# An expert layer on one core: 64 of 256 tokens leave the dense sweep, their rows gathered by index

## The reference, cut to what matters

```python
def block(xb):                      # xb: 128 tokens x 1024
    q = (xb @ w_q).reshape(128, 8, 2, 128)
    s = jnp.einsum('thpd,hpkd->thpk', q, subkeys)            # 128 keys per half
    s1, i1 = lax.top_k(s[:, :, 0], 16)
    s2, i2 = lax.top_k(s[:, :, 1], 16)
    cand = (s1[..., :, None] + s2[..., None, :]).reshape(128, 8, 256)
    cidx = (i1[..., :, None] * 128 + i2[..., None, :]).reshape(128, 8, 256)
    top, pos = lax.top_k(cand, 16)
    idx = jnp.take_along_axis(cidx, pos, axis=-1)            # expert numbers
    g = jax.nn.softmax(top, axis=-1)
    ue, ve = u[idx], v[idx]                                  # rows of 1024
    act = gelu(jnp.einsum('td,thkd->thk', xb, ue))
    return jnp.einsum('thk,thkd->td', g * act, ve)
```

## Time and profile before

| | |
|---|---|
| median of 3 runs | 5376.34 us (5371.48 to 5377.14) |
| the profiled execution | 5365.48 us, span 5363.7 us |
| PE busy | 4796.7 us (89%) |
| DVE / ACT / POOL busy | 3541.7 (66%) / 2498.5 (47%) / 516.1 (10%) |
| moved | 862.62 MB, mean 161 GB/s |
| granted clock, mean | 0.936 |

### The profile page before, as it was taken

One profiled execution on the slowest core, in us unless ns is written; L12 is line 12 of the kernel. 1 busy time (PEld: TensorE's weight loads), 2 busy tenths in 40 slices (PEclk: granted clock), 3 DMA queues, 4 the chain that ended last, 5 costly groups with the idle time before them and its releaser, 6 DMA issues. The chain is left out here.

```text
span 5363.7 us, 94694 instructions
## 1 busy us (share of the span) xinstructions
PE 4796.7 (89%) x35838; PEld 4543.3 (85%) x35838; DVE 3541.7 (66%) x7839; ACT 2498.5 (47%) x4941; POOL 516.1 (10%) x789
## 2 busy tenths in 40 slices
PE   8868999999899999976799999969888988887896
PEld 6647999999899999964799999969778888886896
DVE  7554886588687668845587668846465555537564
ACT  6424554444455544432455444434454444446443
POOL 0000029000005700000005700000000000000000
PEclk9979999999999999988899999989878989978998
DMA  8402664766475467621375476635304444430453
GB/s 306 150 32 68 208 197 127 222 230 229 162 223 169 153 225 229 229 82 45 111 222 169 149 228 228 229 116 186 133 25 148 155 148 148 153 132 33 148 183 105
DMA packets 265098, 862.62 MB, mean 161 GB/s; under 512 B 29328, under 2 KB 32272, under 8 KB 264006
## 3 DMA queue, kind: packets, MB, share of 16 engines
q1 hardware_dynamic: 264070, 854.18, 48.8%
q10 hardware_dynamic: 576, 2.39, 0.1%
HBM read 805.03 MB, written 51.42 MB: 160 GB/s over the span
## 5 line engine op out<-in xcount | busy, mean ns | idle before, releaser
L148 DVE TENSOR_TENSOR weight_lo<-weight_ring,weight_hi 128x512 fp32r<-128x512 f32 x2840 | 1954.9, 692 | 1446.1 <-ACT weight_hi L141 1428.3
L141 ACT ACTIVATE weight_hi<-weight_ring 128x512 fp32r<-128x512 f32 x2840 | 1781.6, 631 | 2396.7 <-PE ffn_gu L173 269.9
L173 PE MATMUL ffn_gu<-second_x_hi,weight_hi 128*128 128x256 f32 x1408 | 399.0, 283 | 37.6 <-PEq L205 37.6
L173 PE MATMUL ffn_gu<-second_x_lo,weight_hi 128*128 128x256 f32 x1408 | 398.3, 283 | 0.0
L173 PE MATMUL ffn_gu<-second_x_hi,weight_lo 128*128 128x256 f32 x1408 | 398.0, 283 | 0.0
L173 PE MATMUL peer10e_dot<-peer_xh,weight_hi 128*128 128x256 f32 x1152 | 334.7, 291 | 13.6 <-PEq L205 9.9
L173 PE MATMUL peer00e_dot<-peer_xh,weight_hi 128*128 128x256 f32 x1152 | 334.6, 290 | 11.7 <-PEq L205 9.9
L173 PE MATMUL peer01e_dot<-peer_xh,weight_hi 128*128 128x256 f32 x1152 | 334.3, 290 | 11.9 <-PEq L205 9.9
L173 PE MATMUL peer00e_dot<-peer_xl,weight_hi 128*128 128x256 f32 x1152 | 326.7, 284 | 0.0
L173 PE MATMUL peer10e_dot<-peer_xl,weight_hi 128*128 128x256 f32 x1152 | 326.7, 284 | 0.0
L173 PE MATMUL peer00e_dot<-peer_xh,weight_lo 128*128 128x256 f32 x1152 | 326.6, 284 | 0.0
(11 more groups left out here) (612 smaller groups left out, 13529.4 us busy)
## 6 DMA issues: line engine op xcount, KB each, us to landing
weight_ring<-in_peer_tiles SPq DMA_DIRECT2D x768, 512.0 KB, 3.8
weight_ring<-in_w_tiles SPq DMA_DIRECT2D x652, 512.0 KB, 3.4
peer_acts<-peer00e_gelu SPq DMA_DIRECT2D x64, 256.0 KB, 4.2
peer00e_act_in<-peer_acts SPq DMA_DIRECT2D x64, 256.0 KB, 3.8
peer_acts<-peer01e_gelu SPq DMA_DIRECT2D x64, 256.0 KB, 4.1
peer01e_act_in<-peer_acts SPq DMA_DIRECT2D x64, 256.0 KB, 4.1
peer_acts<-peer10e_gelu SPq DMA_DIRECT2D x64, 256.0 KB, 4.1
peer10e_act_in<-peer_acts SPq DMA_DIRECT2D x64, 256.0 KB, 3.7
```

Of the source, the lines that this page charges most:

```text
L141: act.activation(self.hi[:, part % PARTS, :], self.ring[:, g % RING, (part % 2) * PART:(part % 2 + 1) * PART], ACT.Copy).then_inc(self.hi_ ...
L148: dve.tensor_tensor(self.lo[:, part % PARTS, :], self.ring[:, g % RING, (part % 2) * PART:(part % 2 + 1) * PART], self.hi[:, part % PARTS, ...
L173: last = pe.matmul(out, lhsT, rhs, start=start and i == 0, stop=stop and i == len(passes) - 1, **more)
```

## The change

- **64 tokens of each stream go another way.** The u and v sweeps take the other 192 (`DENSE`): matmuls of 192 moving columns, 48 groups. The 16 query tiles stay at 256.
- **Rows by index.** The 64 tokens lie twice over the 128 partitions, each copy with half of its 128 choices. After the routing of the first 128 tokens (which now comes first, 82 pieces from step 8) POOL fetches, by indirect DMA, one row of 1024 for each partition: 64 gathers from u, then 64 from v, into three buffers. DVE works on each in one pass of 1024 columns: a dot product with the token (`row`, i < 64), then, after a gelu on ACT, a multiply and add into `rows_sum`. Row i has its place at step `row_step(i)`, spread evenly to the end of the stage. PE adds up the two copies at the end (`fold`).
- **Coefficients on three engines.** POOL multiplies (`weigh`), ACT rounds, DVE takes the remainder. On POOL's queue the gathers, the one-hots and `weigh` are in one order; gather i waits until row i - 3 has been consumed.
- **One-hots**: the softmax weight moves to POOL's; DVE's is one operation of 512 columns a group instead of four of 128.
- **Splits per whole tile**, in all stages: one operation of 1024 columns each on ACT and DVE when PE is through with a tile's second part; three tiles (six parts) are kept.
- At the start of a stage the tokens' sum of hi and lo is written twice by DVE, turned by PE (8 transposes) and copied by ACT to `xt`.

```diff
-PARTS = 4
+PARTS = 6
...
+    def write_hi(self, act, g):
+        if g < len(self.tiles):
             act.wait_ge(self.arrived[g % RING], 16 * (g // RING + 1))
...
+            act.activation(self.tile_of(self.hi, g), self.ring[:, g % RING, :], ACT.Copy).then_inc(self.hi_done, 2)
+
+    def write_lo(self, dve, g):
+        if g < len(self.tiles):
+            dve.wait_ge(self.hi_done, 2 * g + 2)
+            dve.tensor_tensor(self.tile_of(self.lo, g), self.ring[:, g % RING, :],
+                              self.tile_of(self.hi, g).bitcast(F32), ALU.subtract).then_inc(self.lo_done, 2)
...
     def next_hi(self, act, part):
 
-        act.wait_ge(self.used, part + 1)
-        self.write_hi(act, part + PARTS)
+        if part % 2:
+            act.wait_ge(self.used, part + 1)
+            self.write_hi(act, part // 2 + PARTS // 2)
 
     def next_lo(self, dve, part):
 
-        self.write_lo(dve, part + PARTS)
+        if part % 2:
+            self.write_lo(dve, part // 2 + PARTS // 2)
...
+SPARSE = 64
+DENSE = T - SPARSE
+COPIES = P // SPARSE
+ROWS = 3
...
             def routing(step):
-                for c in range(QT):
-                    yield from choose(c)
                 for tt in range(2):
+                    for c in range(0, QT, 2):
+                        yield from choose(tt, c)
                     yield from top_k(tt, step)
-
-            def seconds(g):
+                    if tt == 0:
+                        yield from experts_of()
+                    routed_at.append(step())
...
+        def row_step(i):
+            lead = routed_at[0] + 14
+            return lead + i * (steps - 10 - lead) // (2 * NG) + (6 if i >= NG else 0)
+        def spread_step(g):
+            return routed_at[1] + 8 + g * (2 * front - 6 - routed_at[1] - 8) // groups
...
+                lo = SPARSE + g * GROUP
+                dve.tensor_tensor(second[:, g % 2, :, :], iota.unsqueeze(1).to_broadcast([P, GROUP, P]),
+                                  route[:, 1, lo:lo + GROUP].unsqueeze(2).to_broadcast([P, GROUP, P]),
+                                  ALU.is_equal).then_inc(second_done, 1)
+
+            def row(i):
+                dve.wait_ge(row_arrived[i % ROWS], 16 * (i // ROWS + 1))
+                here, j = rows[:, i % ROWS, :], i % NG
+                if i == 0:
+                    dve.wait_ge(xt_done, 1)
+                if i < NG:
+                    dve.tensor_tensor_reduce(here, here, xt[:, :], 1.0, 0.0, ALU.mult, ALU.add,
+                                             dots[:, j:j + 1]).then_inc(consumed, 1)
+                    return
+                dve.wait_ge(consumed, i)
+                if j == 0:
+                    dve.wait_ge(W.used, 2 * v0)
+                    dve.tensor_scalar(rows_sum, here, share[:, j:j + 1], None, ALU.mult).then_inc(consumed, 1)
+                else:
+                    dve.scalar_tensor_tensor(out=rows_sum, in0=here, scalar=share[:, j:j + 1], in1=rows_sum,
+                                             op0=ALU.mult, op1=ALU.add).then_inc(consumed, 1)
...
+            def rows_until(m):
+                while routed_at and done_rows[0] < 2 * NG and row_step(done_rows[0]) <= m:
+                    if done_rows[0] == NG:
+                        weigh_rows()
+                    row(done_rows[0])
+                    done_rows[0] += 1
+
             for m in range(2 * front):
                 now[0] = m
                 W.next_lo(dve, 2 * q0 + m)
-                if busy and m >= 4:
+                if busy and m >= 8:
                     busy = next(pieces, "done") != "done"
-                    if not busy:
-                        spread_from.append(m + 6)
-                if not busy and 0 <= m + 1 - spread_from[0] < groups:
-                    seconds(m + 1 - spread_from[0])
-            assert spread_from and spread_from[0] + groups + 4 <= 2 * front, spread_from
+                rows_until(m)
+                while not busy and done_groups[0] < groups and spread_step(done_groups[0]) <= m + 1:
+                    one_hots(done_groups[0])
+                    done_groups[0] += 1
+            assert not busy and done_groups[0] == groups
...
             def coef(j):
-                b, slot = j % 2, (j // 2) % ACTS_IN
-                if j == 0:
-                    dve.wait_ge(spread_out, groups)
-                if j % 2 == 0:
-                    dve.wait_ge(act_arrived[slot], 16 * (j // 2 // ACTS_IN + 1))
-                chain.mark(dve.tensor_tensor(weight[:, :], act_in[:, slot, j % 2, :], G[:, j, :], ALU.mult))
-                chain.wait()
-                if j >= 2:
-                    dve.wait_ge(W.used, 2 * (v0 + j - 2) + 2)
-                dve.tensor_copy(coef_hi[:, b, :], weight[:, :]).then_inc(weighed, 1)
-                dve.wait_ge(weighed, j + 1)
-                dve.tensor_tensor(coef_lo[:, b, :], weight[:, :], coef_hi[:, b, :].bitcast(F32),
+                dve.wait_ge(hi_done, j + 1)
+                dve.tensor_tensor(coef_lo[:, j % 2, :], weight[:, j % 2, :], coef_hi[:, j % 2, :].bitcast(F32),
                                   ALU.subtract).then_inc(weighted, 1)
-                dve.wait_ge(weighted, j + 1)
 
             coef(0)
             for m in range(2 * NKEYS):
                 if m % 2 == 0 and m // 2 + 1 < NKEYS:
                     coef(m // 2 + 1)
                 W.next_lo(dve, 2 * v0 + m)
+                rows_until(2 * front + m)
...
         @block.gpsimd
         def _(pool):
-            pool.wait_ge(routed, 2)
-            for g in range(groups):
+            def gather(i):
+                table, j = i // NG, i % NG
+                if i >= ROWS:
+                    pool.wait_ge(consumed, i - ROWS + 1)
+                pool.indirect_dma_start(rows[:, i % ROWS, :], None, (u_rows, v_rows)[table],
+                                        bass.IndirectOffsetOnAxis(ap=pick[:, table, j:j + 1].bitcast(U32), axis=0)
+                                        ).then_inc(row_arrived[i % ROWS], 16)
+
+            def one_hots(g):
+                if g == 0:
+                    pool.wait_ge(routed, 2)
                 if g >= 2:
                     pool.wait_ge(multiplied, g - 1)
                 for t in range(GROUP):
-                    at = g * GROUP + t
-                    last = pool.tensor_scalar(first[:, g % 2, t, :], iota, route[:, 0, at:at + 1], None, ALU.is_equal)
+                    lo = SPARSE + g * GROUP + t
+                    last = pool.tensor_scalar(first[:, g % 2, t, :], iota, route[:, 0, lo:lo + 1], route[:, 2, lo:lo + 1],
+                                              ALU.is_equal, ALU.mult)
                 last.then_inc(first_done, 1)
+
+            def weigh(j):
+                slot = (j // 2) % ACTS_IN
+                if j == 0:
+                    pool.wait_ge(spread_out, groups)
+                if j >= 2:
+                    pool.wait_ge(weighted, j - 1)
+                if j % 2 == 0:
+                    pool.wait_ge(act_arrived[slot], 16 * (j // 2 // ACTS_IN + 1))
+                pool.tensor_tensor(weight[:, j % 2, :], act_in[:, slot, j % 2, :], G[:, j, :], ALU.mult).then_inc(weighed, 1)
+
+            pool.wait_ge(picked_done, 1)
+            for c in range(COPIES):
+                pool.dma_start(pick[c * SPARSE:(c + 1) * SPARSE, :, :], picked[0:SPARSE, :, c * NG:(c + 1) * NG]
+                               ).then_inc(pick_in, 16)
+            pool.wait_ge(pick_in, 16 * COPIES)
+            queued = 0
+            for m in range(steps):
+                while queued < 2 * NG and row_step(max(queued - ROWS, 0)) - (0 if queued >= ROWS else 100) < m:
+                    gather(queued)
+                    queued += 1
+                if m < 2 * front:
+                    for g in spread_steps.get(m + 3, ()):
+                        one_hots(g)
+                    continue
+                if m == 2 * front:
+                    weigh(0)
+                j = (m - 2 * front) // 2 + 1
+                if m % 2 == 0 and j < NKEYS:
+                    weigh(j)
+            assert queued == 2 * NG
 
         @block.tensor
         def _(pe):
+            pe.wait_ge(twice_done, 1)
+            for k in range(KD):
+                last = pe.transpose(flat[:, D + k * P:D + (k + 1) * P],
+                                    x_twice[:, k, :, :].rearrange("p c s -> p (c s)"), ident)
+            last.then_inc(x_turned, 1)
...
@@ in the tensor block @@
-                    last = run_passes(pe, dot[:, n % 2, 0:T], W.stationary(2 * q0 + m, k * P, x(4 * half + k)),
+                    at_k = tuple(b[:, cols] for b in x(4 * half + k))
+                    last = run_passes(pe, dot[:, n % 2, 0:width], W.stationary(2 * q0 + m, k * P, at_k),
...
-                        last = run_passes(pe, acc[:, n, :],
+                        last = run_passes(pe, acc[:, n, 0:DENSE],
...
+                if j == NKEYS - 2:
+                    pe.wait_ge(consumed, 2 * NG)
+                    pe.wait_ge(folded, 1)
```

(44 more changed lines are left out.)

195 lines of the change are left out of this document (124 added, 71 removed).

## The result

| | before | after |
|---|---|---|
| median | 5376.74 us (5371.48 to 5381.41, 4 runs) | 6262.65 us (6258.48 to 6264.99, 4 runs) |
| profiled execution | 5365.48 us, span 5363.7 | 6258.48 us, span 6256.6 |
| fronts of the three expert stages | 510.9 / 511.3 / 514.1 | 595.1 / 592.6 / 598.6 |
| v sweeps | 370.0 / 370.2 / 370.0 | 567.6 / 568.6 / 567.4 |
| all else (span less these) | 2717 | 2767 |

The ratio is 1.165 (95% interval 1.163 to 1.167): slower by 16%. A front runs from the first matmul on `dot` to the first on `acc`, a sweep from there to the last on `acc`. Of the 893 us that the span grew, the sweeps have 593, the fronts 250 and the rest 50.

A forecast was written before the change was run, and what follows sets the result against it. PE was taken as the bound, DVE next at 84%. Three stages of +168 (sweep) and -1 (front), plus 20 and 8, gave +529 on 5365.5; set against the median, 5905 us, from 5665 to 6170, wider range 5600 to 6350.

The forecast's parts named there:

- the upper end that was added up: Whole kernel: gather issue of 2.0 us and fronts 30 us longer give +796, 6170 us.
- Narrow matmul: u and v tiles: a 192-column matmul takes 0.112 us instead of 0.120, saving 147 us in all.
- Splits: All stages: whole-tile splits take 1.22 us on DVE and about 1.1 on ACT; some 20 us at stage ends.
- All hidden in PE's shadow: Whole-tile splits: their time is covered by PE, as two tiles of split weights remain when one is used up.
- The row's chain in the sweep: v sweep: coefficients wait behind split, row and gather; 195 us of stalls, sweep 539 against 371, +168 a stage.
- g: v sweep: POOL's time to issue one gather, taken as 1.2 us, bounds 0.1 to 2.0.
- The clock in the sweep: Rival: narrow matmuls leave the v sweep at 1.2 GHz, 704 us a sweep, 6400 in all; chance 12%.
- Front: Query and u tiles of each expert stage: 509 us against 510, PE's gain given back to DVE.
- The 38 us for one-hots behind the split: Front, steps 169 to 287: PE waits some 1.6 us in each of 24 groups.
- Rest: Outside fronts and sweeps: 20 us at stage ends from splits and 8 at expert stages' starts, 28 us.
- Transfers bind: Rival: at 306 GB/s a v tile needs 3.0 us, 386 a sweep, 5450 in all; chance 8%.
- The rows hidden: Rival: no coefficient waits for rows; sweeps 344, fronts 471, 5205 us in all; chance 8%.

The follow-up runs named there:

- e11: Changed kernel without gathers and row passes, POOL's one-hots at one operation, DVE's one-hots and the sweep's coefficients queued ahead of splits: 5197.11 us.
- e5: Kernel before with only the whole-tile splits, two activation slots instead of three and coefficients laid over the one-hots: 5702.77 us.
- e2: Changed kernel with POOL's coefficient product ahead of the gather in the v sweep, and gathers three steps later: 5774.36 us.
- e3: Changed kernel with the v sweep's odd-step rows moved to the next even step, behind that step's coefficients on DVE: 5982.26 us.
- e4: Changed kernel with the edits of e2 and e3 together: 5681.61 us.
- e1: Changed kernel without gathers and DVE's row passes, so the 64 tokens' experts are missing from the output: 5459.74 us.
- e10: e4 plus its order in the front, e7's edit, sweep coefficients ahead of splits, and POOL's one-hots at one operation: 5339.26 us, 0.994 of the kernel before.
- e12: e10 with splits per half tile again, as in the kernel before: 5287.86 us, 0.984 of the kernel before.
- e7: Changed kernel with DVE's one-hots of a step queued ahead of that step's split: 6207.57 us.

## Why the prediction was right, and where not

The direction, the sweep's mechanism and its place were right. The time, 6263, is 358 above the number and 93 above the upper end that was added up, 6170; it is inside the range to 6350 only by the allowance for a partial fall of the clock, which had no price. Against the profiled execution's +893 stand +529: sweeps +593 for 504, fronts +250 for -3, the rest +50 for 28. So 253 of the 364 us missed are the fronts, where a term was left out; that the total still came inside is in part luck.

- **Narrow matmul: right.** At the full clock they start 0.111 to 0.112 us apart, taken as 0.112. At 1.2 GHz it is 0.213, the 0.212 that 48 columns had shown: the floor a matmul is there at 192 columns too. e11's sweep, 347.5, is this term alone (344 forecast).
- **Splits: 1.23 and 1.06** for 1.22 and 1.1, right. "All hidden in PE's shadow" was not: e5 says that alone they cost 332 us. I worked out their depth only where rows or one-hots stood behind them, and left it out for a sweep without rows.
- **The row's chain in the sweep: right.** Forecast 6.55 us from tile to matmul and 3.86 of waiting for an odd step; the timeline has 6.3 and 3.70. The gather's issue, g, the largest unknown, was 1.07 for 1.2. e2 and e3 each take away one of the two things it consists of, e4 both: 568 to 408, 479 and 374.
- **The clock in the sweep: a rival's part came true.** The forecast gave 12% to a full fall and wrote that part may happen, at no price. 711 of the first sweep's matmuls start 0.200 to 0.230 us apart (151.7 us, where 0.112 would make 80): 72 us. The 88 distances above 0.23 hold 145 us of pause for the 195 forecast, as a slow tile covers more of the chain: 15 tiles ran at least 20 of their matmuls at 1.2 GHz, and 14 of them were followed by no distance above 0.21. 344 + 145 + 72 + some 7 of small ones is 568 for 539. The rival's ground, that narrow matmuls do not bring the clock up, fell: in e1, e4 and e10 they run at 0.99. Nor did the argument against the rival hold, that pauses behind a low clock were longer than 4 us: the longest distance in this sweep is 3.98. It is the pauses; without them the clock stayed.
- **Front: the step that failed.** Steps 0 to 103 took 154.5 for 153, steps 104 to 168 101.1 for 115 (my estimate of DVE's load was too high by the row's share). Steps 169 to 287 took 339.5 for 241. The 38 us for one-hots behind the split were near (48.5 us, 26 times, for 24 times 1.6). Missing were POOL and the clock. POOL: I had read 600 ns for its one-hot, and the diff moves the factor onto it: two operations are 793. In addition its mean is 1075 beside DVE (below), and gathers that wait for rows stand ahead of it: 4 x 1.075 + 1.2 a gather, 34 in 48 groups, is 5.2 us a group before any waiting, 248 us, already more than the 241 I gave the whole stretch. I named this queue and gave it 30 us at the upper end, without that sum. The clock: PE's waits for the products are 82 us for the 38, and with them the stretch ran at 0.87, where the kernel before had 1.00 (window, columns as above):
```profile
776.00:1115.00 339.00, 247.21 (x1813) 240.56 (x1811) 152.60 (x192) 103.27 (x171) 247.78 (x231) 0.87 0.56 174
```
  Outside all its pauses (92 us) PE took 248 us for the work of this stretch, and 207 in e11, where the clock is 1.00. So of the 98 us missed some 54 are pauses and 41 are the clock (an estimate from these two runs); in the sum it stood at nothing, here as in the sweep. e10, with POOL at one operation and nothing waiting ahead, takes 244.3.
- **Rest: right in kind,** 28 forecast, 50 measured; e5 and e12 show that 38 come and go with the splits (20 forecast), the other 12 are the stages' starts (8).
- **Transfers bind: fell.** I took 306 GB/s as the most; e10's sweep moves 331. The rows hidden: e10 is that rival, in another order of the same work, at 5339 for its 5205; its fronts are 504 in the mean for 471, its sweeps 353 for 344, the rest is the 50 for 28.

Of the 192 one-hots after the change, the 124 that met no DVE operation of two tensors and over 0.5 us took 791 ns in the mean and at most 808; the 68 that met one took 1592, the longest 3445. The mean of all is 987 without rows (e1), 1075 with them, 1228 in e7, where they follow each other with 1.5 us of idle time in all. The Trainium skill (SBUF — State Buffer, SBUF: two separate sides) says of the port that DVE and GpSimd share that, when DVE's operation has two inputs in SBUF, the first to start holds it for the whole instruction and the other "fully blocks". The runs agree with it.

## What to carry to other kernels

A queue is served in order, so an instruction that waits for a late event (a gather for a freed buffer) belongs behind those that others wait for, and a large instruction costs its length to everything that is queued behind it even where its engine is half idle: coarser splits saved DVE 0.15 us a tile and took 332 us from the kernel before. When work moves to another engine, add up that engine's own queue over the stretch, with the operation's new form, before calling it hidden. And two causes that hold the same stretch show little when they are taken away singly: here 8 and 35 us a front, together 91. Pauses also have a price beyond their length where the clock falls with them: some 72 us in the first sweep and 41 in the first front here.

## What the runs showed that was not expected

- GpSimd's one-hot over 128 columns is 0.60 us with one operation and 0.79 with two.
- 128 rows by index take 1.0 us of POOL to issue when it is undisturbed (0.98, 1.00 in the timelines), 1.78 at the mean in e4.
- PE's pauses brought its clock down with them. The first sweep after the change has 35 distances of over 2 us between matmuls and 19 of 0.5 to 2, and stood 170 us at 1.2 GHz; e3's has 12 and 39, and 67 to 85 us in its three; e2's has none and 37, and 4 us.
